# Split matrix products that read the moving operand and write PSUM from the last column to the first

## The reference

```python
def swiglu(h, w_in, w_out):
    gate, up = jnp.split(h @ w_in, 2, axis=-1)
    return (jax.nn.silu(gate) * up) @ w_out

def hybrid_layer(x, w_in, ...):
    h = rms_norm(x, norm_w)
    p = h @ w_in
    ...
    proj = jnp.einsum('bsgc,gcd->bsgd', branches, w_branch)
    gates = jax.nn.sigmoid(merge.reshape(...))
    mixed = jnp.sum(gates * proj, axis=2)
    return x + (mixed @ w_out).astype(x.dtype)
```

## Time and profile before

| | |
|---|---|
| runs | 2421.0, 2419.41, 2419.73 us |
| median | 2419.73 us |
| span of the profiled execution | 2419.5 us, 0.2 us below the median of the runs |
| PE busy | 2384.9 us, 14,712 matmuls |
| VectorE busy | 1600.1 us |
| ScalarE busy | 1063.2 us |
| HBM read | 343.14 MB, 142 GB/s over the span |

### The profile page before, as it was taken

One profiled execution on the slowest core, in us unless ns is written; L12 is line 12 of the kernel. 1 busy time (PEld: TensorE's weight loads), 2 busy tenths in 40 slices (PEclk: granted clock), 3 DMA queues, 4 the chain that ended last, 5 costly groups with the idle time before them and its releaser, 6 DMA issues.

```text
span 2419.5 us, 36353 instructions
## 1 busy us (share of the span) xinstructions
PE 2384.9 (99%) x14712; PEld 2059.6 (85%) x14712; DVE 1600.1 (66%) x2899; ACT 1063.2 (44%) x1882; POOL 0.2 (0%) x4
## 2 busy tenths in 40 slices
PE   9999999999999999999999999999999999999998
PEld 5888888976788888888888888899998998999997
DVE  7776775477587677377623357655586776877767
ACT  4222324455552223252223245644556556555663
POOL 0000000000000000000000000000000000000000
PEclk9999999999999999999999999999999999999999
DMA  6554552211125455215522212245534443444432
GB/s 275 207 195 188 202 198 70 88 53 53 71 91 197 186 198 203 87 55 207 207 107 90 102 70 88 111 157 181 191 142 157 175 140 127 167 169 158 157 123 88
DMA packets 48408, 346.53 MB, mean 143 GB/s; under 512 B 5361, under 2 KB 5489, under 8 KB 6769
## 3 DMA queue, kind: packets, MB, share of 16 engines
q1 hardware_dynamic: 48242, 344.21, 38.3%
HBM read 343.14 MB, written 1.05 MB: 142 GB/s over the span
## 4 chain that ended last, share of the span: by engine, by line
PE 92%; DVE 5%; ACT 2%; issue 1%; DMA 0%; SPq 0%; DVEq 0%; ACTq 0%
PE ps L484 26%; PE ps L485 25%; PE ps L486 25%; PE ps L826 1%; PE ps L828 1%; PE ps L827 1%; DVE w_lo L2119 1%; PE ps L873 1%; PE ps L1030 1%; PE ps L654 1%; ACT w_hi L1430 1%; PE ps L679 1%; PE ps L1056 1%; PE ps L859 1%; PE ps L608 1%
## 5 line engine op out<-in xcount | busy, mean ns | idle before, releaser
L1430 ACT ACTIVATE w_hi<-ring 128x1024 fp32r<-128x1024 f32 x494 | 523.4, 1060 | 1052.5 <-PE ps L486 988.9
L2119 DVE TENSOR_TENSOR w_lo<-ring,w_hi 128x1024 fp32r<-128x1024 f32 x494 | 603.5, 1223 | 422.8 <-ACT w_hi L1430 419.5
L484 PE MATMUL ps<-u_hi,w_hi 128*128 128x512 f32 (+1 forms) x1856 | 656.8, 354 | 4.8 <-DVE u_lo L2192 2.3
L485 PE MATMUL ps<-u_lo,w_hi 128*128 128x512 f32 (+1 forms) x1856 | 648.6, 349 | 0.0
L486 PE MATMUL ps<-u_hi,w_lo 128*128 128x512 f32 (+1 forms) x1856 | 648.4, 349 | 0.0
L484 PEld LDWEIGHTS ps<-u_hi,w_hi 128*128 128x128 f32 x1856 | 348.4, 188 | 60.9 <-issue 7.7
L485 PEld LDWEIGHTS ps<-u_lo,w_hi 128*128 128x128 f32 x1856 | 348.5, 188 | 47.3 <-issue 0.5
L486 PEld LDWEIGHTS ps<-u_hi,w_lo 128*128 128x128 f32 x1856 | 348.6, 188 | 45.5
L484 PE MATMUL ps<-uh,w_hi 128*128 128x256 f32 x1136 | 321.9, 283 | 2.9 <-DVE w_lo L2119 1.7
L2107 DVE CUSTOM_DVE_ANT_0 waste<-ring,condb,cols 128x1024 f32<-128x1024 f32 x260 | 322.3, 1279 | 0.1
L486 PE MATMUL ps<-uh,w_lo 128*128 128x256 f32 x1136 | 315.4, 278 | 0.0
(11 more groups left out here) (364 smaller groups left out, 2686.6 us busy)
## 6 DMA issues: line engine op xcount, KB each, us to landing
ring<-in_wk SPq DMA_DIRECT2D x317, 1024.0 KB, 4.8
mix<-in_wk SPq DMA_DIRECT2D x3, 1024.0 KB, 16.2
yT<-in_wk SPq DMA_DIRECT2D x2, 1024.0 KB, 7.8
hT<-in_x SPq DMA_DIRECT2D x1, 2048.0 KB, 13.1
htabs<-in_htabs SPq DMA_DIRECT2D x1, 1088.0 KB, 7.3
out_t<-uT SPq DMA_DIRECT2D x2, 512.0 KB, 2.6
trig<-in_trig SPq DMA_DIRECT2D x3, 256.0 KB, 7.5
wuk<-in_uk SPq DMA_DIRECT2D x2, 256.0 KB, 5.1
```

The lines of the kernel that those rows point to most:

```text
L484: mm(bank, hi, x_hi, start=first, stop=False, skip_group_check=skip)
L485: mm(bank, hi, x_lo, start=False, stop=False, skip_group_check=skip)
L1430: f(half_hi(K, 0, HALF), ringed(n, K % 2 * HALF, (K % 2 + 1) * HALF), ACT.Copy).then_inc(whi_ready, 1)
L2119: tt(half_lo(K, 0, HALF), ringed(HALF_SLOT[K], K % 2 * HALF, (K % 2 + 1) * HALF), half_hi(K, 0, HALF).bitcast(F32), ALU.subtract).then_inc ...
```

## The change

In `three`, one line is added ahead of the three matmuls. The views of the output bank and of the moving operands (hi and lo) are replaced by the same columns with a step of -1. Input column i still goes to output column i; the operands of the stationary side are as before. No other matmul is changed.

```diff
             def three(bank, hi, lo, x_hi, x_lo, first, last, skip=False):
 
+                bank, x_hi, x_lo = bank[:, ::-1], x_hi[:, ::-1], x_lo[:, ::-1]
                 mm(bank, hi, x_hi, start=first, stop=False, skip_group_check=skip)
                 mm(bank, hi, x_lo, start=False, stop=False, skip_group_check=skip)
                 return mm(bank, lo, x_hi, start=False, stop=last, skip_group_check=skip)
```

## The result

The changed kernel takes 2461.7 us (2460.87 to 2462.91, four runs) against 2419.57 us (2418.47 to 2421.0, four runs): 1.0175 times as long, 95% interval 1.0161 to 1.019, or 42 us. The time lies in the stated range, but the forecast was no change, and it is slower by a small amount clear of noise. The price is neither 0 nor the 1778 us of half rate. It is small and comes with each matmul, as in Rival 2, but is four times what that rival allowed.

The account below looks back on a forecast made before the run. TensorE was taken to bound the kernel; the change was priced at 0 on a 2419.5 us span, and the shown runs' median, +0.2 us, gave 2419.7 us. The 8-in-10 range was 2412 to 4220 us, reaching to half rate.

Parts of the forecast that it names:

- Rival 2: Each matmul of `three` takes one more pair of columns, 0.86 ns, as a fixed step: 2430 us; chance 6%.
- What bounds the kernel: TensorE bounds it, 92% of the chain of waits; any cost in `three` goes into the time almost one for one.
- Counts and part of the kernel touched: Only the 11,928 matmuls of `three` change, 4824 over 512 columns and 7104 over 256; plain float32 and lines 826 to 828 stay.
- The price, taken as 0: Extra time of a matmul in `three` that reads and writes downwards: 0 ns, so 2419.7 us; chance 60%.
- the 11.1 and 15.0 ns beyond the columns: Time per matmul of `three` above 0.417 ns a column: 11.1 ns at 256 columns, 15.0 at 512, called the fixed part.
- Groups visited whole, so no difference: In `three`, the downward walk visits the same aligned groups of two or four words, each once, so it costs nothing.
- Rival 1: Downward moving read or PSUM write in `three` runs at half rate: +1778 us, 4150 to 4220 us; chance 31%.
- Rival 3: Matmuls of `three` get faster by losing time beyond the columns, at most 151 us; one ns gives 2408 us; chance 3%.
- What the profile would show: Starts of triples in `three` still 685 ns apart at 512 columns and 353 at 256; other spacings named for two rivals.

Follow-up runs that it names:

- e4_place: Kernel before, all reads and writes upwards, with only the activations moved on by 64 bytes: 2453.99 us, 1.0142 times the kernel before.
- bench1: Separate small kernel, TensorE alone, stretches of 48 matmuls up or down: at 512 columns 11.20 us with the read down, 10.89 us with the write alone down.
- e8_u12: Kernel before, all upwards, with only `u_hi` and `u_lo` of the first model starting 48 bytes later: 2416.57 us, 0.9983 times the kernel before.
- e6_base: Kernel before, all upwards, with every buffer, weights and activations alike, moved on by 64 bytes: 2421.15 us, 1.0003 times the kernel before.
- e7_by12: Kernel before, all upwards, with all six split buffers of the activations starting 48 bytes later: 2428.83 us, 1.0034 times the kernel before.

## Why the prediction was wrong, point by point

- **What bounds the kernel** held. 42.8 us more of PE became 42 us of time; ScalarE's wait grew by 43.7 us.
- **Counts and part of the kernel touched** held: the loss lies in the 11,928 matmuls of `three`, and lines 826 to 828 and the plain float32 ones did not move beyond 2 us in sum.
- **The price, taken as 0, was the step that failed.** It measured 43.3 us / 11,928 = 3.6 ns a matmul: 4.3 at 512 columns, 3.2 at 256. Two readings led there. First, line 1322 stood as the neighbour which shows that the place of a run doesn't matter; but it is plain float32, at half the pace, and such matmuls show neither direction (215.8 ns both) nor any step. `e4_place` loses 34 us by place alone. Secondly, the 11.1 and 15.0 ns beyond the columns were called a fixed part, as if nothing could move it. They are 6.7 and 13.3 ns a matmul at the best pace, and 0 to 20 ns a triple of steps on top; rows 7 beside a stretch ten microseconds on would have shown it.
- **Groups visited whole, so no difference**, the reason given for the 0, fits that half rate did not occur (Rival 1: undisturbed triples take 700 ns, not 1322) and is silent on the steps. With the read alone turned round, the same groups in the opposite order cost the whole 42 us (`e1_read`). By the Trainium skill's page "SBUF — State Buffer" (the note on 16-byte cachelines) four hits a line should run at full rate; the runs show 120.0 and 233.3 ns against 113.3 and 226.7 at best. The measurement decides: for float32r at the 2.4 GHz level the direction matters though every line is used whole. The Trainium skill's page "Advanced Engine Details and Errata" (PSUM Cachelines) holds in the mild reading: with a step of -1 into PSUM alone the time is 1.0003 times as long (`e2_write`).
- **Rival 2** had the right form, a small step per instruction, the right sign and the deciding point (0.4 ns). Its size, 0.86 ns, came from a guess at one pair of columns and was four times too small; with 6% it was given too little. It is no fixed step either: in `bench1` it is 1.0 ns at 128 columns, 4.4 at 384 and -1.5 at 256.
- **Rival 3's bound** (151 us in what lies beyond the columns) was the right place to look, on the wrong side: the change lost there, and `e8_u12` could win no more than 4.4 us, 0.17% of the time.
- **What the profile would show**: 229.2 and 118.7 ns were named for Rival 2; 233.3 and 120.0 came.

**What stays open.** Why an upward read sometimes saves a step and a downward one does not. The mutual place of moving run and stationary tile decides (`e6_base` against `e4_place`), which speaks against what the Trainium skill's page "TensorE: Matmul & The Clock Gate" says of two independent read ports (the step on loading the stationary operand); but with fewer stationary columns the walk down is no faster at 512 columns, and the price remains without a following load, so a clash of the two reads is argued, not shown. Over how many bytes the effect of the place repeats is open as well: 128 is ruled out (226.7 ns at 0, 232.6 at 128), 256 was not tried in a stretch. A stationary tile that lies reversed in SBUF, with the columns of the weights packed the other way round, was not tried.

## What to carry to other kernels

Where TensorE streams float32r at its upper clock and nothing else bounds the kernel, the wrong direction or mutual place of the operands cost 1 to 2% here; the best placement that was tried won 0.17%. Both cost nothing to try: read the moving operand upwards, and time a few placements of the split buffers. A small kernel can stand for the large one only if every pair of operands lies in it as in the large one; here a count modulo 128 bytes was too coarse, and three forecasts leaned on stretches of another place. Take no mean pace from one stretch: compare the distance between starts in several stretches of the same shape, and where it comes in steps, ask what sets the number of steps before calling it a fixed part. A neighbouring row that runs at half the demand is no evidence on a limit of supply.

## What the runs showed of the hardware

- Undisturbed float32r triples at the 2.4 GHz level take 687 ns at 512 columns and mostly 340 or 353 at 256 in the kernel before, 700 and 360 in the changed one: steps of 6.67 ns over 680 and 340, up to three. Other places have other cycles: 690 to 706 ns (`e4_place`), 363 to 370 (`e7_by12`). At the 1.2 GHz level no step was seen (213.3 ns a matmul at 256 columns, up and down).
- Reversing the read costs 13 ns a triple at 512 columns and 7 or 20 at 256 in this kernel (1.0177), reversing the write into PSUM nothing that can be told apart (1.0003).
- Moving the activations by 64 bytes against the weights cost 34 us (1.0142), moving both by 64 bytes nothing that can be told apart (1.0003).
- At the same mutual place a stream of 512-column triples has the same cycle in a small kernel and in the large one, to the nanosecond (705, 691, 704, 695, 690, 705, 690).
